# Reordering the jobs of TensorE and the evictions behind them in a fused hybrid decoder layer

## What is computed

```
u = rmsnorm(x)
A) mLSTM, 4 heads            q,k = silu(conv(u@Wq|Wk)); v, o, gates from u;  h_ml = norm(mlstm(...)) * sigmoid(o)
B) sparse attention, 8 heads q = rope(norm(u@Wq)); compressed keys/values = two-layer net over blocks of 32 tokens,
                             k2 = rope(norm(.));  compressed + selected + window attention -> h_nsa
C) cross-attention, 4 heads  softmax(q k^T) v over 256 memory tokens -> h_mem
merged = sum_b sigmoid(u@Wgate_b) * (h_b @ W_b)          b = ml, nsa, mem
x = x + merged @ W_out
x = x + MoE(rmsnorm(x))      32 experts, top 4 per token, each expert 1024 -> 2*1024 -> 1024
```

## Time and profile before

| | |
|---|---|
| device time, median of 3 runs | 1291.0 us (1289.5 to 1292.44) |
| the profiled execution: its own time, its span | 1292.44 us, 1290.5 us |
| PE (TensorE) busy | 1124.7 us, 87% |
| VectorE / ScalarE busy | 269.6 us, 21% / 216.9 us, 17% |
| mean granted clock of TensorE | 0.926 of full |
| DMA moved | 455.63 MB, 353 GB/s over the span |

### The profile page before, as it was taken

How to read it: one execution, slowest core, us unless ns; L and a number is a source line. 1 busy time by engine, 2 the same in 40 slices (tenths; PEclk the granted TensorE clock), 3 DMA queues, 4 the chain that set the end, 5 groups by cost and what they waited for, 6 DMA issues and landing times.

```text
span 1290.5 us, 19299 instructions
## 1 busy us (share of the span) xinstructions
PE 1124.7 (87%) x7511; PEld 534.5 (41%) x7512; DVE 269.6 (21%) x728; ACT 216.9 (17%) x486; POOL 17.4 (1%) x24
## 2 busy tenths in 40 slices
PE   8999999999999996679967855999596969699967
PEld 4665868888444332123321321333231323144412
DVE  3235452562141110001110100111010101011101
ACT  2116432362021110011100100111010101011101
POOL 1100000000000000000000000000000000000000
PEclk9999999999999997679987977899898979799978
DMA  9933336524699999999999999969999999999996
GB/s 328 358 110 128 131 132 260 200 90 172 238 390 411 427 425 424 425 426 427 426 426 427 426 426 426 426 261 426 428 425 425 425 426 426 428 426 426 426 427 262
DMA packets 66886, 455.63 MB, mean 353 GB/s; under 512 B 7588, under 2 KB 13576, under 8 KB 34088
## 3 DMA queue, kind: packets, MB, share of 16 engines
q1 hardware_dynamic: 66344, 454.48, 85.8%
q10 hardware_dynamic: 448, 0.60, 0.1%
q0 software_dynamic: 64, 0.13, 0.0%
HBM read 454.15 MB, written 1.05 MB: 353 GB/s over the span
## 4 chain that ended last, share of the span: by engine, by line
PE 65%; DMA 25%; SPq 7%; issue 1%; DVE 1%; ACT 0%; ACTq 0%; DVEq 0%
DMA mq<-in_b_gu 22%; PE bank L1095 17%; PE bank L1120 10%; PE bank L590 6%; PE bank L731 6%; PE bank L1046 4%; SPq L394 4%; PE bank L1054 3%; PE bank L1074 3%; DMA mem<-in_w_down 3%; SPq L510 3%; PE bank L893 2%; PE bank L639 2%; PE bank L927 2%; PE bank L579 2%
## 5 line engine op out<-in xcount | busy, mean ns | idle before, releaser
L1095 PE MATMUL bank<-mem 128*32 128x512 f32 x2944 | 358.2, 628 | 149.7 <-DMA mq<-in_b_gu 149.3
L1095 PEld LDWEIGHTS bank<-mem 128*32 128x32 f32 x2944 | 94.4, 113 | 359.9 <-issue 356.9
L1120 PE MATMUL bank<-mem 128*32 128x512 f32 x1472 | 180.1, 629 | 2.4 <-issue 1.6
L1854 DVE TENSOR_SCALAR mem<-bank 128x256 f32<-128x256 f32 x46 | 19.5, 425 | 745.2 <-PE bank L1095 745.2
L1422 ACT ACTIVATE mq<-bank 64x512 f32<-64x512 f32 x46 | 27.1, 589 | 465.8 <-PE bank L1120 465.8
L1120 PEld LDWEIGHTS bank<-mem 128*32 128x32 f32 x1472 | 45.2, 115 | 139.5 <-issue 138.0
L1046 PEld LDWEIGHTS bank<-mem,sc 128*128 128x128 f32 x736 | 83.9, 192 | 19.2 <-issue 19.2
L1046 PE MATMUL bank<-mem,sc 128*128 128x64 f32 x736 | 87.1, 277 | 0.0
L590 PE MATMUL bank<-mem 128*128 128x512 f32 x192 | 83.4, 592 | 0.0
L1054 PE MATMUL bank<-mq,mem 128*128 128x512 f32 x176 | 81.4, 605 | 0.0
L731 PE MATMUL bank<-mem 128*128 128x256 f32 x320 | 71.6, 381 | 0.0
(11 more groups left out here) (306 smaller groups left out, 781.9 us busy)
## 6 DMA issues: line engine op xcount, KB each, us to landing
mem<-in_w_gu SPq DMA_DIRECT2D x128, 2048.0 KB, 32.7
mem<-in_w_down SPq DMA_DIRECT2D x64, 2048.0 KB, 36.2
mem<-in_w_in SPq DMA_DIRECT2D x13, 2048.0 KB, 12.4
mem<-in_w_out SPq DMA_DIRECT2D x2, 2048.0 KB, 8.5
mem<-in_w_mem_kv SPq DMA_DIRECT2D x2, 1024.0 KB, 7.1
mem<-in_w_mem_kv SPq DMA_DIRECT2D x1, 2048.0 KB, 8.1
mem<-in_cmp_w_k SPq DMA_DIRECT2D x1, 2048.0 KB, 8.4
mem<-in_cmp_w_v SPq DMA_DIRECT2D x1, 2048.0 KB, 9.5
```

The source lines that it names most:

```text
L1095: mm = nc.tensor.matmul(BH[n][32 * s:32 * s + 32, :], xgT[:, k, 32 * n:32 * n + 32], w[:, c, 512 * s:512 * s + 512], start=k == 0, stop=k ...
L1120: mm = nc.tensor.matmul(BG[64 * hh + 32 * two:64 * hh + 32 * two + 32, :], actT[:, o:o + 32], w[:, 2 * c + two, 512 * hh:512 * hh + 512], ...
```

## The change

Five reorderings; no matmul, copy or load is added or removed. (1) In cross-attention TensorE issues turn 0, scores 2, turn 1, scores 3, out 0, nq0, nq1, ngate, turn 2, turn 3, out 1; ScalarE and VectorE follow that order. (2) `nkv` is computed and evicted before `kcvc`, with the chunks swapped; ScalarE gets one wait more, for `hml_ready`, ahead of the copies of `kcvc`. (3) The transpose `kcT` moves behind the projection `bgl11`. (4) In the step of head 3 `nsa_exp(5)` comes ahead of the sigmoid of `bgn00`, and at heads 4, 6 and 7 that sigmoid has the wait for `pm11` too. (5) The job list follows, so banks change among the jobs moved.

```diff
-... ("bgm1", "bgm11"), ("kcvc", "kcvc"), ("nkv", "nkv1"), ("w1k", "hk"), ...
+... ("bgm1", "bgm11"), ("nkv", "nkv1"), ("kcvc", "kcvc"), ("w1k", "hk"), ...
-    jobs += ["mP0", "mP1", "ms2", "ms3", "nq0", "mo0", "mP2", "mP3", "nq1", "mo1", "ngate"]
+    jobs += ["mP0", "ms2", "mP1", "ms3", "mo0", "nq0", "nq1", "ngate", "mP2", "mP3", "mo1"]
@@ TensorE
             mem_turn(0)
+            mem_scores(2)
             mem_turn(1)
-            mem_scores(2)
             mem_scores(3)
-            natural([(0, "nq0")], slot3("nq", KT, 512), 512)
             mem_out(0)
+            natural([(i, f"nq{i}") for i in range(NT)], slot3("nq", KT, 512), 512)
+            (ngate)
             mem_turn(2)
             mem_turn(3)
-            natural([(1, "nq1")], slot3("nq", KT, 512), 512)
             mem_out(1)
-            (ngate)
...
+            natural([(i, f"nkv{i}") for i in range(NT)], slot3("nkv", KT, 512), 512)
             (kcvc)
-            natural([(i, f"nkv{i}") for i in range(NT)], slot3("nkv", KT, 512), 512)
...
             bgate("bgl", 1, 0)
+            bgate("bgl", 1, 1)
             pe.wait_ge(S("kc_roped"), 1)
             transposes("kcT", [(0, kcn[0:30, :])])
-            bgate("bgl", 1, 1)
@@ ScalarE
             mem_turned(0)
+            mem_exp(2)
             mem_turned(1)
-            mem_exp(2)
             mem_exp(3)
-            copy nq0
             copy mo0
+            copy nq0, copy nq1, sigmoid ngate
             mem_turned(2)
             mem_turned(3)
-            copy nq1
             copy mo1
-            sigmoid ngate
...
+            copy nkv0, copy nkv1
+            act.wait_ge(S("hml_ready"), 1)
             (eight copies of kcvc)
-            copy nkv0, copy nkv1
...
             gate("bgl", bg1, 1, 0)
+            gate("bgl", bg1, 1, 1)
             copy("kcT", kcT, bank("kcT")[:, 0:30])
-            gate("bgl", bg1, 1, 1)
...
                 nsa_turned(h)
-                if h == 3:
-                    was_read(act, "pm11")
-                    gate("bgn", bg0, 0, 0)
                 if h + 2 < QH:
                     nsa_exp(h + 2)
-                if h in (4, 6, 7):
+                if h in (3, 4, 6, 7):
+                    was_read(act, "pm11")
                     (gate "bgn")
@@ VectorE
             mem_norm(0)
-            mem_norm(1)
             arrived(dve, "gT")
             (two copies of gT)
             mem_max(2)
+            mem_norm(1)
             mem_max(3)
```

More of the change, by code:

```diff
@@ L88, in job_order @@
     jobs += ["mkT0", "mkT1", "v0", "v1", "gw", "mqT0", "mqT1", "gif", "ms0", "ms1", "o0", "o1", "gT"]
-    jobs += ["mP0", "mP1", "ms2", "ms3", "nq0", "mo0", "mP2", "mP3", "nq1", "mo1", "ngate"]
+    jobs += ["mP0", "ms2", "mP1", "ms3", "mo0", "nq0", "nq1", "ngate", "mP2", "mP3", "mo1"]
     jobs += ["ST0", "MB0", "bgm00", "ST1", "MB1", "num0", "bgm01", "ST2", "MB2", "num1",
              "bgm10", "ST3", "MB3", "num2", "bgm11", "num3"]
-    jobs += ["kcvc", "nkv0", "nkv1", "nqT0", "nqT1", "hmlT0", "hmlT1", "hk", "hv"]
-    jobs += ["bgl00", "hkT", "hvT", "bgl01", "nkT0", "nkT1", "kc", "vc", "bgl10", "kcT", "bgl11"]
+    jobs += ["nkv0", "nkv1", "kcvc", "nqT0", "nqT1", "hmlT0", "hmlT1", "hk", "hv"]
+    jobs += ["bgl00", "hkT", "hvT", "bgl01", "nkT0", "nkT1", "kc", "vc", "bgl10", "bgl11", "kcT"]
     jobs += ["sA0", "sB0", "sA1", "sB1"]
@@ L691, in _ @@
             mem_turn(0)
+            mem_scores(2)
             mem_turn(1)
-            mem_scores(2)
             mem_scores(3)
-            natural([(0, "nq0")], slot3("nq", KT, 512), 512)
             mem_out(0)
-            mem_turn(2)
-            mem_turn(3)
-            natural([(1, "nq1")], slot3("nq", KT, 512), 512)
-            mem_out(1)
+            natural([(i, f"nq{i}") for i in range(NT)], slot3("nq", KT, 512), 512)
             b = begin("ngate")
@@ L704, in _ @@
             done(mm, "ngate")
+            mem_turn(2)
+            mem_turn(3)
+            mem_out(1)
             def ml_scores(h):
@@ L1278, in _ @@
             mem_turned(0)
+            mem_exp(2)
             mem_turned(1)
-            mem_exp(2)
             mem_exp(3)
-            copy("nq0", nq_sb[:, 0, :], bank("nq0")[:, :])
             arrived(act, "mkT1")
             copy("mo0", heads[:, 0, 0:2, :], bank("mo0")[:, :].rearrange("p (h t) -> p h t", h=2))
+            for i in range(NT):
+                copy(f"nq{i}", nq_sb[:, i, :], bank(f"nq{i}")[:, :])
+            arrived(act, "ngate")
+            read(nc.scalar.activation(gsb[:, :, :].rearrange("p i n -> p (i n)"), bank("ngate")[:, 0:48], ACT.Sigmoid), "ngate")
             mem_turned(2)
             mem_turned(3)
-            copy("nq1", nq_sb[:, 1, :], bank("nq1")[:, :])
             copy("mo1", heads[:, 1, 0:2, :], bank("mo1")[:, :].rearrange("p (h t) -> p h t", h=2))
-            arrived(act, "ngate")
-            read(nc.scalar.activation(gsb[:, :, :].rearrange("p i n -> p (i n)"), bank("ngate")[:, 0:48], ACT.Sigmoid), "ngate")
             def gate(name, dst, hh, j):
@@ L1320, in _ @@
             nc.scalar.activation(sp_[:, 0:1024], hml.rearrange("p i h e -> p (i h e)"), ACT.Square).then_inc(S("h_sq"), 1)
+            for i in range(NT):
+                copy(f"nkv{i}", nkv[:, i, :], bank(f"nkv{i}")[:, :])
+            act.wait_ge(S("hml_ready"), 1)
             arrived(act, "kcvc")
@@ L1327, in _ @@
             read(ins, "kcvc")
-            for i in range(NT):
-                copy(f"nkv{i}", nkv[:, i, :], bank(f"nkv{i}")[:, :])
             arrived(act, "mo1")
```

## The result

The changed kernel takes 1302.19 us (median; 1299.77 to 1308.0, 6 runs), the kernel before 1291.09 us (1289.5 to 1292.44, 6 runs): ratio 1.008, 95% interval 1.006 to 1.0098, that is 10.3 us slower (7.7 to 12.7). A second comparison on another chip gave 1.0077 (1.0064 to 1.009), 9.9 us. Eight further executions of the changed kernel took 1298.87 to 1301.77 us, so that the 1303.9 to 1308.0 of three of the six stand alone; I have no account of them. The prediction was 7.4 us, 1298.4 us against the median.

What follows compares the result with a forecast made beforehand. TensorE bounds the trunk without idle time, then saturated weight DMA, so trunk delays reach the end whole. Stalls of 1.97 + 1.59 + 2.7 + 0.57 + 0.57 = 7.4 us give 1298.4 us against the median, range 1294.5 to 1302.5.

Steps and rivals of the forecast that it cites:

- Turn 1 behind scores 2: Cross-attention: TensorE stands 1.97 us until VectorE, needing scores 2 first, has finished its reduction and normalisation.
- Out 1: Cross-attention: TensorE waits 1.59 us while ScalarE does nq1's copy, a table load and ngate before copying mP2.
- hk behind kcvc: Ahead of hk: TensorE waits 2.7 us for eight kcvc copies and two of four additions, formerly hidden under nkv.
- the key rotations ahead of nkT: VectorE's key rotations start later but finish at 213.6, before TensorE needs them at 215.2: hidden, 1.6 us left.
- The late table load: Sigmoid with two waits: table load comes only after the bank arrives, 1.28 us late at heads 4 and 6, covered by filler.
- kcT behind bgl11: First attention scores: TensorE waits 0.57 us for the kcT copy, since ScalarE evicts bgl11 first.
- The exponentials ahead of the sigmoid: Scores of heads 6 and 7: bank 3 is free at 278.65, before at 277.05, so TensorE waits 0.57 us.
- The rule weighed against a row: Table switches: the skill adds about 1.38 us of draining each, making the sum 10.2 us; the forecast followed the profile row, without draining.
- Partly covered: Rival: one of the three large stalls is absent; about 4 us slower, 1295 us; chance 0.14.
- Absorbed: Rival: the weight stream hangs on fixed load order, so a trunk 7 us later costs nothing, 1291 us; chance 0.06.
- Faster: Rival: busy TensorE hides waits at heads 3 to 7 and earlier exponentials pay off, 1287 us; chance 0.04.
- The clock falls too: Rival: the 2.7 us stall halves the clock for hk and hv, 11 us in all, 1302; with table drain, chance 0.06.

Runs made afterwards that it cites:

- pure delay: The kernel before with 21 extra dummy matmuls ahead of the mLSTM scores; ratio 1.0078 to the kernel before, 10.1 us slower.
- fillers: The changed kernel with dummy matmuls in two TensorE waits, 3 ahead of turn 1 and 4 ahead of hk; 1.0068, again 1.0071, against the kernel before.
- parts 3 and 4 alone: The kernel before with only kcT behind bgl11 and head 5's exponentials ahead of the sigmoid with its longer waits; 1.0018, 2.3 us slower.

## Why the prediction was right, and where it was off

*What bounds the kernel* held. A trunk without idle time had nothing to give, and a delay of the trunk reaches the end at some 89% (pure delay, 10.1 of 11.3 us, with an interval of 8.0 to 12.1).

*Turn 1 behind scores 2*, forecast 1.97 us, measured 1.98. *Out 1*: 1.59, measured 1.52. *hk behind kcvc*: 2.7, measured 2.81. Each was a chain of rows of other engines, and all held to about a tenth of a microsecond. The costs put at nothing held as well: the added wait, the key rotations ahead of nkT, the queue of SyncE.

*The late table load* came as forecast at head 4. ScalarE before, with one wait ahead of the sigmoid, then in the changed kernel, with two:

```profile
284.47 1.28 ACT L1296 ACT_TABLE_LOAD   x1
287.13 0.60 ACT L1296 ACTIVATE mem<-bank 128x512 f32<-128x512 f32 x1 [1.39 <-PE bank L893]
...
299.26 1.28 ACT L1295 ACT_TABLE_LOAD   x1 [2.77 <-PE bank L892]
300.56 0.60 ACT L1295 ACTIVATE mem<-bank 128x512 f32<-128x512 f32 x1
```

With one wait the load lies ahead of the idle time, with two behind it, and the sigmoid comes 1.3 us later. No wait of TensorE came of it here.

*kcT behind bgl11*: 0.57, measured 1.12. The term left out that TensorE still had four met waits to work off. *The exponentials ahead of the sigmoid*: 0.57, measured 0.8: the bank is free when I said, and TensorE starts 0.25 us behind the end of the sigmoid; that this is the same effect, with waits for banks behind the one for `sA7`, I only argue.

*The sum* was 7.4 us; the waits alone came to 8.2, and the trunk grew by 12.0 in the first profile and by 10.4 in the second. The step that failed is "the matmuls themselves sum to the same". It held the clock at full behind each stall, on the strength of one window in the expert loop (6.74 of 10 us busy, clock 1.00). I didn't look at the single waits in that window. They are these:

```profile
382.05 0.51 PE L1105 MATMUL bank<-mem 128*128 128x128 f32 x2 [1.59 <-DVE w_it L1872]
...
388.98 2.31 PE L1120 MATMUL bank<-mem 128*32 128x512 f32 x17 [1.55 <-issue]
```

Neither is as long as the stalls of 2.0 and 2.7 us that I forecast. The next longer wait in that profile is 5.6 us, and the matmuls behind it run at 1.2 GHz, so the window said nothing of the sizes in question. I had the fall as a rival at hk alone, with 3.6 us; it came at turn 1 too, and measured 1.9 and 1.76 us where it came. The range of 1294.5 to 1302.5 just held the 1302.19 us, and that is in part luck: its upper end was made of dearer handshakes at all five places and of late key rotations. Two handshakes were dearer, by 0.6 and 0.2 us, the rotations cost nothing, and the clock took that room. My forecast proper of 6 to 9 us, with 0.70, was too low; 10 us and more had 0.06.

*The rule weighed against a row*: the wait ahead of out 1 fell by 1.2 us when a table load of 1.28 us and a sigmoid left it, so the row was right, and the draining of the Trainium skill (ScalarE: Activation LUTs, What ACT_TABLE_LOAD costs) isn't seen here. *The rule of the rival*, that an idle array is put to half rate (the Trainium skill, TensorE: Matmul & The Clock Gate, Part 1: The HAM clock gate), is borne out by the fillers and the count: 5 of 10 unfilled stalls brought the clock down, and in the 18 cases without one it stayed up. Here a wait of 2.0 us did it in 2 of 5 profiles.

*Rivals.* "Partly covered" is out, since all five waits came. "Absorbed" is out by the pure delay. "Faster" is out: the earlier exponentials brought nothing (parts 3 and 4 alone: 1.86 us in the trunk, all loss). "The clock falls too" is what filled the gap.

## What to carry to other kernels

Where one engine has no idle time, a reordering can only cost; price it job by job as the chain on the other engines between the last operand and the job, and count the table load and every met wait that stands behind the last one. Then add that the first microseconds behind each new wait may run at half clock: here some 1.7 us a place, in 5 of the 10 cases profiled. To judge that risk from a profile, read the single waits in it, not the busy share of a window. And don't compare two spans to better than a few microseconds where a stretch begins behind a long wait: the moment at which the clock returns is the execution's, not the kernel's.

## What the runs showed that I had not expected

- A wait of 2.0 us on TensorE is enough to bring the clock from 2.4 to 1.2 GHz, in 2 of 5 profiles; one of 2.8 us in 3 of 5. The waits of 1.5, 1.1 and 0.8 us did not in the profiles read here.
- Waits that are already met cost TensorE about 0.1 us each when they stand behind the wait that ends last (1.12 us with four of them behind it, 0.69 with four ahead, one profile).
- A table load of ScalarE runs ahead of one wait but behind the second of two: 284.47 us, ahead of 1.39 us idle, against 299.26, behind 2.77 us idle.
- Fillers in a wait bring the clock back to full (window 1.00 for 0.61 and 0.70) and 1.7 to 3.4 us in the trunk, of which the side-by-side timing shows 0.8 us, inside its uncertainty.
